# A diffusion trunk on one core: convolution and output product in one block, squares a stage ahead, norms inside the next product stage

## The chip, the core and the metric

The kernel runs on one core of a Trainium2 chip. The metric is the device time of one execution in microseconds (us); several executions are timed and the median is given. TensorE (PE) multiplies matrices, VectorE (DVE) and ScalarE (ACT) do elementwise work, GpSimd (POOL) does a little of it and issues gathers, SyncE (SP) issues transfers. The engines run their own instruction streams and meet at semaphores.

## The reference, cut to what matters

The input is 512 latent tokens and 256 context tokens of 1024 channels, in float32. There are two layers. Each layer is a token mixer followed by a retrieval of experts, and around each stands the same frame:

```python
def rms_norm(x, g):
    xf = x.astype(jnp.float32)
    y = xf * lax.rsqrt(jnp.mean(xf * xf, axis=-1, keepdims=True) + RMS_EPS)
    return (y * g.astype(jnp.float32)).astype(x.dtype)

def modulate(h, shift, scale):
    return h * (1 + scale) + shift
...
def short_conv_mixer(h, w_in, k, w_out, rows):
    gate_b, gate_c, v = jnp.split(h @ w_in, 3, axis=-1)
    z = gate_c * v
    ...
    return (gate_b * zc) @ w_out
...
        hx = modulate(rms_norm(x, norm1_g[i]), mx[0], mx[1])
        ...
        x = x + mx[2] * yx
        x = x + mx[5] * peer_ffn(modulate(rms_norm(x, norm2_g[i]), mx[3], mx[4]),
                                 peer_w_q[i], peer_keys[i], peer_u[i], peer_v[i])
```

The mixer of layer 0 is the short convolution above, that of layer 1 a gated linear recurrence (HGRN2) with eight heads. The experts are found by ranking scores of queries against 128 keys per list, 16 lists a token; the shifts, scales and gates (`mx`, `mc`) come from a product of a condition vector with `ada_w`, 6144 values for each layer and each of the two kinds of token. The output is the final RMS norm of the latent tokens.

## The kernel before, in words

The residual stream `xT` stays in SBUF, channels on the 128 partitions, as 8 slices (k) of 768 tokens (512 in the second half of layer 1). Every big product is taken from weights in tiles of 128 output channels. A tile's weights are loaded to one of four slots (`t.load`, line 129), copied to a rounded high part by ScalarE (`t.hi`, line 133), and the rest is subtracted into a low part by GpSimd or VectorE (`t.lo`, line 144). `t.product` (line 159) then multiplies high by high, high by low and low by high for each k and each bank of up to 512 tokens: 48 matmuls for a tile of 768 tokens. Two accumulators in PSUM alternate; a product waits for `acc_free`, which whoever reads the accumulator out raises. Two sets of split weights alternate too.

The kernel is a sequence of stages. Each stage is a block, and no engine starts the next before all have ended this one:

- `stage_front` (line 199): constants, the modulation of layer 0, the first norm.
- `stage_conv` (line 513): 24 tiles (n), three for each of eight channel slices c, in the order gate c, v, gate b. A loop of two turns has twelve tiles written out in each. ScalarE copies the first accumulator (line 578), VectorE multiplies the second onto it (z, line 616), applies three taps (lines 623 and 632), multiplies the third (y, line 638) and subtracts the part that ScalarE rounded (y_hi, line 583) to get y_lo (line 643). Between these steps VectorE also takes the modulation of layer 1: 48 rows, six for each c, three after z and three after y_lo. A row is 1024 weights on each partition; two dot products (line 608) reduce it against the two condition vectors, with a transfer of 512 KB into one of six slots ahead of it. `acc_free` of the third accumulator is raised at line 641.
- `stage_mix_out` (line 660): eight tiles of the output product. ScalarE copies each accumulator (line 696) and VectorE adds it, scaled, to `xT` (line 717). In layer 1 it first splits the heads' output, and the first product follows this slice by slice.
- `stage_norm` (line 414): squares of the eight slices by ScalarE (line 441) and VectorE (line 468) in turn, sums over partitions by a product of each with a matrix of ones (line 458), root (line 443), reciprocal (line 470). Then VectorE scales each slice (line 484), ScalarE adds the shift and rounds it to `h_hi` (line 450), and VectorE subtracts to get `h_lo` (line 494). It stands three times between other stages (before the first ranking, the recurrence and the second ranking), and a form of it ends the kernel, with the scaled output stored (lines 474 and 504).
- `stage_rank` (line 725): loads the keys (line 751), waits for them (line 763), takes the first query product, then turns the summed h of the sparse tokens (`turn_h`, line 765; ScalarE's copy is line 820) and goes through 16 lists: product, scores, ranks by VectorE.
- `stage_gates` (line 874): dense products against all experts and the gates' matrices. It is not touched.
- `stage_experts` (line 1265): 128 tiles accumulated in all eight PSUM banks, while VectorE adds gathered rows for the sparse tokens. At its end VectorE adds the eight accumulators to `xT` (line 1442), TensorE turns the row sums (line 1364) and VectorE adds these (line 1449).
- `retire` (line 106), after layer 0: GpSimd clears the semaphores used so far.
- `stage_hgrn` (line 1457): the recurrence, 40 tiles, five for each head. Its first five products stand before the loop over heads.

The order around the change is written out by hand, in each engine's stream. Waits are counted in turns; nothing is planned by a program.

Of the kernel before, what the change touches and what calls it, by code (L numbers as in the profile page):

```python
# [23 lines left out]
P = 128  # L24
D = 1024
# [388 lines left out]
def stage_norm(t, layer, n, tokens):  # L414

    nc = t.nc
    final = n == 2
    tag = f"n{layer}{n}"
    hv = banks(tokens)
    segs = [(0, SEQ, 0)] + ([(SEQ, CTX, 1)] if tokens == TOK else [])  # L420
    with ExitStack() as ctx:
        sb = lambda nm, s, d=F32: ctx.enter_context(nc.sbuf_tensor(nm + tag, s, d))
        sq = sb("sq", [P, 2, tokens])
        rs = sb("rs", [P, tokens])
        rstd = sb("rstd", [P, tokens])
        xn = sb("xn", [P, 3, tokens])
        out = sb("out", [P, KC, tokens]) if final else None
        sq_done = [t.sem(f"sq{s}{tag}") for s in ("_act", "_dve")]
        sum_part, root, rstd_done = (t.sem(s + tag) for s in ("sums", "root", "rstd"))
        xn_done, hi_done, lo_done = (t.sem(s + tag) for s in ("xn_", "hi_", "lo_"))  # L430
        stored = t.sem("stored" + tag) if final else None
        h_hi, h_lo = (t.h_hi, t.hc_hi), (t.h_lo, t.hc_lo)
        shift = lambda k, c: t.mod[:, layer, c, 24 * n + k:24 * n + k + 1]
        with nc.Block() as block:  # L434

            @block.scalar
            def _(act):
                for k in range(0, KC, 2):
                    if k >= 2:
                        act.wait_ge(sum_part, k - 1)  # L440
                    act.activation(sq[:, 0], t.xT[:, k, 0:tokens], ACT.Square).then_inc(sq_done[0], 1)  # L441
                act.wait_ge(sum_part, KC)
                act.activation(rs[:], t.acc(0, tokens), ACT.Sqrt, bias=t.eps[:],  # L443
                               scale=1.0 / D).then_inc(root, 1)
                if final:
                    return
                for k in range(KC):
                    act.wait_ge(xn_done, len(segs) * (k + 1))
                    for t0, w, c in segs:
                        act.activation(h_hi[c][:, k], xn[:, k % 3, t0:t0 + w], ACT.Identity,  # L450
                                       bias=shift(k, c)).then_inc(hi_done, 1)

            @block.tensor
            def _(pe):
                for k in range(KC):
                    pe.wait_ge(sq_done[k % 2], k // 2 + 1)
                    for i, (t0, w) in enumerate(hv):
                        last = pe.matmul(t.psum[:, i, 0:w], t.ones[:], sq[:, k % 2, t0:t0 + w],  # L458
                                         start=(k == 0), stop=(k == KC - 1))
                    last.then_inc(sum_part, 1)  # L460

            @block.vector
            def _(dve):
                for k in range(1, KC, 2):
                    if k >= 2:
                        dve.wait_ge(sum_part, k - 1)
                    x = t.xT[:, k, 0:tokens]
                    dve.tensor_tensor(sq[:, 1], x, x, ALU.mult).then_inc(sq_done[1], 1)
# [3 lines left out]
                if final:  # L472
                    for k in range(KC):
                        dve.scalar_tensor_tensor(out=out[:, k], in0=t.xT[:, k, 0:tokens],  # L474
                                                 scalar=t.gains[:, 4, k:k + 1], in1=rstd[:], op0=ALU.mult,
                                                 op1=ALU.mult).then_inc(xn_done, 1)
                    return
# [1463 lines left out]
```

## Time and profile before

| | us |
|---|---|
| median of three executions | 4391.62 |
| lowest, highest | 4388.56, 4394.60 |
| the profiled execution's own time | 4389.09 |
| its span in the profile | 4387.4 |
| mean granted TensorE clock | 0.956 of full |

One execution was recorded. Its span runs from the first to the last instruction; the time has some 2 us around it. Times in rows of a timeline are us from the start of the span: first the start, then the duration (of several instructions of one kind in a row, from the first start to the last end), then engine and line of the kernel, the operation, what it writes and reads, and in brackets how long the engine had been idle and what released it. A name such as DVEq or PEq as the releaser is that engine's sequencer, so a wait for a semaphore or a barrier.

### The profile page before, as it was taken

What the parts mean: (1) busy time and instruction counts of PE and PEld (TensorE: products, weight loads), DVE (VectorE), ACT (ScalarE), POOL (GpSimd) and SP (SyncE); (2) the same over time, 40 slices, a digit from 0 to 9 for tenths busy, and PEclk for the clock granted to TensorE, in tenths of its full rate; (3) what the DMA queues carried; (4) which work ended last, traced back from release to release, by engine and by line L of the source; (5) the groups of instructions that cost most, each with busy time, mean ns of one, the idle gap of its engine ahead of it and who ended that gap; (6) DMA issues with size and microseconds to landing.
All of it is one profiled execution on the core that took longest, in us unless ns stands there. A gap on an engine that the chain in (4) does not pass through costs nothing. (4 is left out here: it accounts for less than half of the span.)

```text
span 4387.4 us, 62475 instructions
## 1 busy us (share of the span) xinstructions
PE 4032.8 (92%) x20380; PEld 3434.4 (78%) x20380; DVE 3231.5 (74%) x5929; ACT 1947.7 (44%) x3694; POOL 1163.9 (27%) x906
## 2 busy tenths in 40 slices
PE   8997788999999989999987999888799999899998
PEld 2776577788888868888866877656789999899997
DVE  2694588999897778888875455546887877577777
ACT  2111224777777722222224434323367778533332
POOL 0232121343343244444422111112122222122221
PEclk9998899999999999999998999889899999999999
DMA  7441115899999899999951111012378888899996
GB/s 278 169 168 58 44 43 183 284 326 335 318 344 332 316 386 375 373 374 376 376 196 49 38 38 39 29 48 77 123 270 285 285 281 300 293 333 333 331 336 213
DMA packets 411888, 1026.08 MB, mean 234 GB/s; under 512 B 33968, under 2 KB 182448, under 8 KB 405680
## 3 DMA queue, kind: packets, MB, share of 16 engines
q1 hardware_dynamic: 297648, 608.42, 39.0%
q0 software_dynamic: 110592, 402.70, 25.7%
q10 hardware_dynamic: 3456, 12.58, 0.9%
q8 instruction: 98, 1.61, 0.1%
q14 instruction: 94, 0.77, 0.1%
HBM read 904.03 MB, written 119.54 MB: 233 GB/s over the span
## 5 line engine op out<-in xcount | busy, mean ns | idle before, releaser
L136 ACT ACTIVATE w_hi<-w_raw 128x1024 fp32r<-128x1024 f32 x536 | 568.1, 1060 | 1197.9 <-PE psum L1354 879.8
L168 PE MATMUL psum<-h_hi,w_hi 128*128 128x512 f32 (+1 forms) x2208 | 876.4, 397 | 140.3 <-DMA keysr<-in_peer_keys 50.0
L169 PE MATMUL psum<-h_lo,w_hi 128*128 128x512 f32 (+1 forms) x2208 | 840.4, 381 | 0.0
L170 PE MATMUL psum<-h_hi,w_lo 128*128 128x512 f32 (+1 forms) x2208 | 839.7, 380 | 0.0
L147 DVE TENSOR_TENSOR w_lo<-w_raw,w_hi 128x1024 fp32r<-128x1024 f32 x424 | 519.5, 1225 | 413.3 <-ACT w_hi L136 392.2
L1352 PE MATMUL psum<-a_hie,w_hi 128*128 128x512 f32 (+1 forms) x2048 | 764.4, 373 | 30.7 <-DVE a_loe L1407 30.7
L1354 PE MATMUL psum<-a_hie,w_lo 128*128 128x512 f32 (+1 forms) x2048 | 751.6, 367 | 0.0
L1353 PE MATMUL psum<-a_loe,w_hi 128*128 128x512 f32 (+1 forms) x2048 | 750.0, 366 | 0.0
L1228 POOL DMA_INDIRECT u_rowsg<-in_peer_u_rows,expert_idx x384 | 443.4, 1155 | 1099.9 <-DVE u_rowsg L985 974.2
L1333 POOL DMA_INDIRECT v_rowse<-in_peer_v,expert_idx x384 | 421.4, 1097 | 828.2 <-DVE row_sume L1416 815.0
L1160 ACT ACTIVATE ojg<-eq_jg,gate_Tg 128x128 fp32r<-128x128 bf16 x1792 | 546.9, 388 | 167.5 <-DVE eq_jg L1008 166.6
L147 POOL TENSOR_TENSOR w_lo<-w_raw,w_hi 128x1024 fp32r<-128x1024 f32 x116 | 289.4, 2495 | 1145.2 <-ACT w_hi L136 1145.2
L168 PEld LDWEIGHTS psum<-h_hi,w_hi 128*128 128x128 f32 x2208 | 425.9, 193 | 195.5 <-issue 84.4
L1416 DVE SCALAR_TENSOR_TENSOR row_sume<-v_rowse,expert_weight,row_sume 128x1024 f32<-128x1024 f32 x384 | 491.4, 1280 | 0.1
L170 PEld LDWEIGHTS psum<-h_hi,w_lo 128*128 128x128 f32 x2208 | 424.3, 192 | 64.8
L985 DVE SCALAR_TENSOR_TENSOR u_rowsg<-u_rowsg,psum 128x1024 f32<-128x1024 f32 x384 | 463.1, 1216 | 9.5 <-DMA u_rowsg<-in_peer_u_rows,expert_idx 6.4
L169 PEld LDWEIGHTS psum<-h_lo,w_hi 128*128 128x128 f32 x2208 | 425.8, 193 | 49.0 <-issue 12.9
L1352 PEld LDWEIGHTS psum<-a_hie,w_hi 128*128 128x128 f32 x2048 | 385.7, 188 | 93.6 <-DVE a_loe L1407 31.8
L1354 PEld LDWEIGHTS psum<-a_hie,w_lo 128*128 128x128 f32 x2048 | 385.7, 188 | 50.4
L1353 PEld LDWEIGHTS psum<-a_loe,w_hi 128*128 128x128 f32 x2048 | 386.1, 189 | 45.9
L1124 PEld LDWEIGHTS psum<-ojg,eq_ig 128*128 128x128 f32 x1792 | 230.9, 192 | 78.8 <-ACT ojg L1160 70.1
L1124 PE MATMUL psum<-ojg,eq_ig 128*128 128x128 f32 x1792 | 232.6, 273 | 50.1 <-ACT ojg L1160 49.9
(228 smaller groups left out, 5740.2 us busy)
## 6 DMA issues: line engine op xcount, KB each, us to landing
w_raw<-in_peer_u SPq DMA_DIRECT2D x256, 512.0 KB, 5.9
w_raw<-in_peer_v SPq DMA_DIRECT2D x256, 512.0 KB, 5.5
gates<-stageg SPq DMA_DIRECT2D x28, 2048.0 KB, 15.7
acts<-act_gg SPq DMA_DIRECT2D x128, 256.0 KB, 5.0
gte<-gates SPq DMA_DIRECT2D x32, 1024.0 KB, 8.3
act_fe<-acts SPq DMA_DIRECT2D x128, 256.0 KB, 6.3
ada_w<-in_ada_w SPq DMA_DIRECT2D x12, 2048.0 KB, 8.2
ada_rows<-in_ada_w SPq DMA_DIRECT2D x48, 512.0 KB, 3.4
```

Source lines behind the costliest of these rows:

```text
L136: act.activation(self.weights(s)[0], self.raw[:, slot, :], ACT.Copy).then_inc(self.hi_done, 1)
L147: pool.tensor_tensor(lo, self.raw[:, slot, :], hi.bitcast(F32), ALU.subtract).then_inc(self.lo_done, 1)
L168: pe.matmul(out, wh, hi[:, k], start=(k == 0), stop=False)
L169: pe.matmul(out, wh, lo[:, k], start=False, stop=False)
L170: last = pe.matmul(out, wl, hi[:, k], start=False, stop=(k == KC - 1))
L985: dve.scalar_tensor_tensor(out=row, in0=row, scalar=1.0, in1=h_row, op0=ALU.mult, op1=ALU.mult, accum_out=pre_act[:, s, r:r + 1]).then_inc ...
L1124: last = pe.matmul(t.psum[:, 4 + g % 2, j * P:(j + 1) * P], eq_i[:, g % EQ, j], oj[:, g % OJ, x, j], start=(x == 0), stop=(x == 1))
L1160: last = act.activation(oj[:, g % OJ, x, j], eq_j[:, g % EQ, j], ACT.Copy, scale=gate_T[:, b % 2, x, r + j:r + j + 1])
L1352: pe.matmul(out, vh, a_hi[:, s], start=(begin and i == 0), stop=False)
L1353: pe.matmul(out, vh, a_lo[:, s], start=False, stop=False)
L1354: last = pe.matmul(out, vl, a_hi[:, s], start=False, stop=(end and i == QUAD - 1))
L1416: dve.scalar_tensor_tensor(out=acc[:, s], in0=vbuf[:, slot], scalar=weight[:, s, bass.ds(c, 1)], in1=acc[:, s], op0=ALU.mult, op1=ALU.add) ...
```

## The change

It has five parts.

1. **Convolution and output product in one block.** `stage_conv` takes N = 32 tiles: 24 as before, then the eight of the output product, the first of them slice by slice behind y_lo. The loops are written out. `stage_mix_out` is no longer called in layer 0.
2. **Modulation rows spread over both.** Four rows for each channel slice (two for the last, and two behind it), then 3, 3, 3, 3, 2, 2, 0, 0 rows in the eight output tiles: 48 as before. One bias addition and the two scale computations stand behind the last row.
3. **Squares taken a stage ahead.** A new class `Squares` lets ScalarE square each slice of `xT` once it has been added to, and VectorE add the squares up; a single product with ones gives the totals. `stage_experts` squares too, but sums with a product for each slice.
4. **Norms applied in the next product stage.** A new class `Normed` holds root, reciprocal, scaling and rounding. `stage_rank` and `stage_hgrn` call it at their start, and their first product waits for each slice.
5. **The turning of h** in `stage_rank` moves from behind the first product into the last four lists. The wait for the keys moves behind the first product.

The core of the diff:

```diff
+class Normed:
+    def scalar(self, act):
+
+        act.activation(self.rs, self.sums, ACT.Sqrt, bias=self.t.eps[:], scale=1.0 / D).then_inc(self.root, 1)
+        for k in range(KC):
+            act.wait_ge(self.xn_done, len(self.segs) * (k + 1))
+            for t0, w, c in self.segs:
+                act.activation(self.h_hi[c][:, k], self.xn[k % 3][:, t0:t0 + w], ACT.Identity,
+                               bias=self.shift(k, c)).then_inc(self.hi_done, 1)
...
+    def ready(self, pe, k):
+        pe.wait_ge(self.lo_done, len(self.segs) * (k + 1))
+
+class Squares:
+    def square(self, act, added, m, count):
+
+        act.wait_ge(added, count)
+        if m >= 3:
+            act.wait_ge(self.ss_done, m - 2)
+        act.activation(self.sq[m % 2] if m else self.ss[:], self.t.xT[:, m, 0:self.tokens],
+                       ACT.Square).then_inc(self.sq_done, 1)
+
+    def add(self, dve, m):
+
+        dve.wait_ge(self.sq_done, m + 1)
+        if m > 1:
+            dve.wait_ge(self.ss_done, m - 1)
+        dve.tensor_tensor(self.ss[:], self.ss[:], self.sq[m % 2], ALU.add).then_inc(self.ss_done, 1)
+
+    def total(self, pe):
+
+        pe.wait_ge(self.ss_done, KC - 1)
+        for b, (t0, w) in enumerate(banks(self.tokens)):
+            pe.matmul(self.t.psum[:, 6 + b, 0:w], self.t.ones[:], self.ss[:, t0:t0 + w], start=True, stop=True)
...
@@ stage_conv
+    ROWS_C = 4
+    ROWS_M = (3, 3, 3, 3, 2, 2, 0, 0)
...
+                for i in range(n):
+                    t.product(pe, i, i % SPLIT, t.moving(T))
+                for k in range(KC):
+                    pe.wait_ge(ylo_done, k + 2)
+                    t.product(pe, n, n % SPLIT, y_moving, [k])
+                for i in range(n + 1, N):
+                    t.product(pe, i, i % SPLIT, y_moving)
+                squares.total(pe)
...
+                def mixed(m):
+                    t.wait_product(act, n + m)
+                    if m >= 2:
+                        act.wait_ge(added, 2 * (m - 1))
+                    act.activation(tmp[m % 2], t.acc((n + m) % SPLIT, T), ACT.Copy).then_inc(copied, 1)
+                    act.wait_ge(copied, m + 1)
+                    act.sem_inc(t.acc_free[(n + m) % SPLIT], 1)
+                    if m:
+                        squares.square(act, added, m - 1, 2 * m)
...
+                    ada(ROWS_C // 2)
+                ada(ROWS_C // 2)
+                for m in range(KC):
+                    dve.wait_ge(copied, m + 1)
+                    for t0, w, c in segs:
+                        dve.scalar_tensor_tensor(out=t.xT[:, m, t0:t0 + w], in0=tmp[m % 2][:, t0:t0 + w],
+                                                 scalar=t.mod[:, 0, c, 16 + m:17 + m], in1=t.xT[:, m, t0:t0 + w],
+                                                 op0=ALU.mult, op1=ALU.add).then_inc(added, 1)
+                    if m >= 2:
+                        squares.add(dve, m - 1)
+                    if ROWS_M[m]:
+                        ada(ROWS_M[m])
...
@@ stage_rank, TensorE
-                pe.wait_ge(k_in, 16)
...
-                t.product(pe, 0, 0, t.moving(tokens))
-                turn_h(pe)
+                for k in range(KC):
+                    norm.ready(pe, k)
+                    t.product(pe, 0, 0, t.moving(tokens), [k])
+                pe.wait_ge(k_in, 16)
...
                 for i in range(n - BODY, n):
+                    if i - (n - BODY) < S:
+                        turn_h(i - (n - BODY))
                     if i + 1 < n:
                         t.product(pe, i + 1, (i + 1) % SPLIT, t.moving(tokens))
...
@@ stage_experts, TensorE
+                for d in range(KC):
+                    if d == 3:
+                        for s in range(S):
+                            turn(s)
+                    total(d, sq[:, d % 2], sums[:, 0:Td])
+                for d in range(KC):
+                    total(KC + d, sq_rows[:, d % 2].rearrange("p s x -> p (s x)"), sums[:, Td:tokens])
...
@@ stage_hgrn, TensorE
-                for i in range(PER):
+                for k in range(KC):
+                    norm.ready(pe, k)
+                    tile(0, 0, 0, [k])
+                for i in range(1, PER):
                     tile(0, 0, i)
```

`Normed.vector` is the part of `stage_norm` from line 469 to line 496, unchanged. In the recurrence its five buffers are buffers that the first head does not need yet.

## Rows read from the trace of the kernel before

**Rows 1.** The page: busy time of each engine.

```profile
PE 4032.8 (92%) x20380; PEld 3434.4 (78%) x20380; DVE 3231.5 (74%) x5929; ACT 1947.7 (44%) x3694; POOL 1163.9 (27%) x906
```

**Rows 2.** Timeline of TensorE: start us, us, engine line op, [idle before].

```profile
117.95 0.79 PE L168 MATMUL psum<-h_hi,w_hi 128*128 128x512 f32 x1 [4.26 <-PEq L238]
...
364.34 0.76 PE L168 MATMUL psum<-y_hi,w_hi 128*128 128x512 f32 x1 [22.51 <-PEq L542]
...
482.93 0.79 PE L168 MATMUL psum<-h_hi,w_hi 128*128 128x512 f32 x1 [29.32 <-DMA keysr<-in_peer_keys]
...
492.88 1.04 PE L771 MATMUL psum<-ident,h_sumr 128*128 128x128 f32 x8
...
495.94 0.48 PE L168 MATMUL psum<-h_hi,w_hi 128*128 128x512 f32 x1
...
2991.67 0.48 PE L168 MATMUL psum<-h_hi,w_hi 128*128 128x512 f32 x1
```

**Rows 3.** Waits of TensorE, 118 to 364 us: us, times, longest.

```profile
PE psum L168 <- DVEq L641: 13.5, 7, 3.4
```

**Rows 4.** Groups of VectorE, 118 to 364 us: the dot products of the modulation.

```profile
L608 DVE CUSTOM_DVE_ANT_0 ada_rows<-ada_rows,cond_rows 128x1024 f32<-128x1024 f32 x48 | 97.9, 2040 | 0.0
...
L608 DVE CUSTOM_DVE_ANT_0 ada_product<-ada_rows,cond_rows 128x1024 f32<-128x1024 f32 x48 | 63.9, 1331 | 9.7 <-DVE ada_dots L608 6.0 <-DVE z L616 3.8
```

**Rows 5.** Timeline of VectorE, and one row of GpSimd, convolution and output product.

```profile
136.94 0.96 DVE L616 TENSOR_TENSOR z<-gate_c,psum 128x768 f32<-128x768 f32 x1 [22.00 <-PE psum L170]
...
142.44 1.23 DVE L608 CUSTOM_DVE_ANT_0 ada_product<-ada_rows,cond_rows 128x1024 f32<-128x1024 f32 x1 [0.19 <-DVE ada_dots L608]
...
145.01 1.23 DVE L608 CUSTOM_DVE_ANT_0 ada_product<-ada_rows,cond_rows 128x1024 f32<-128x1024 f32 x1 [0.19 <-DVE ada_dots L608]
...
349.28 0.62 DVE L623 TENSOR_SCALAR zc<-z,kern 128x768 f32<-128x768 f32 x1
...
354.49 0.96 DVE L643 TENSOR_TENSOR y_lo<-y,y_hi 128x768 f32 x1 [1.03 <-ACT y_hi L583]
...
385.95 2.69 DVE L717 SCALAR_TENSOR_TENSOR xT<-mix,mod,xT 128x512 f32<-128x512 f32 x2 [5.79 <-ACT mix L696]
...
385.30 2.39 POOL L147 TENSOR_TENSOR w_lo<-w_raw,w_hi 128x1024 fp32r<-128x1024 f32 x1 [6.09 <-ACT w_hi L136]
```

**Rows 6.** Windows: us, busy of five engines, PEclk, DMA, at the output product's start.

```profile
364.00:368.00 4.00, 3.66 (x11) 3.11 (x12) 0.00 (x0) 0.00 (x0) 0.00 (x0) 0.50 0.71 247
...
370.00:372.00 2.00, 2.00 (x13) 1.73 (x12) 0.00 (x0) 0.00 (x0) 0.00 (x0) 1.00 0.00 0
```

**Rows 7.** Timelines of ScalarE and VectorE around the first norm.

```profile
450.58 1.28 ACT L443 ACT_TABLE_LOAD   x1
...
454.58 4.95 DVE L470 RECIPROCAL rstdn<-rsn 128x768 f32<-128x768 f32 x1 [2.58 <-ACT rsn L443]
...
476.74 0.48 DVE L494 SCALAR_TENSOR_TENSOR hc_lop<-xnn,mod,hc_hip 128x256 fp32r<-128x256 f32 x1
```

**Rows 8.** The same around the norm ahead of the recurrence.

```profile
2268.99 5.36 DVE L1442 SCALAR_TENSOR_TENSOR xT<-psum,mod,xT 128x512 f32<-128x512 f32 x8 [3.44 <-PE psum L1354]
...
2285.46 0.96 DVE L468 TENSOR_TENSOR sqn<-xT 128x768 f32<-128x768 f32 x1 [6.98 <-PEq L108]
...
2300.61 4.95 DVE L470 RECIPROCAL rstdn<-rsn 128x768 f32<-128x768 f32 x1 [2.58 <-ACT rsn L443]
...
2335.36 0.81 ACT L1679 ACTIVATE f<-psum 128x768 f32<-128x768 f32 x1 [10.34 <-PE psum L170]
```

**Rows 9.** VectorE around the norm ahead of the second ranking.

```profile
2948.67 2.45 DVE L717 SCALAR_TENSOR_TENSOR xT<-mix,mod,xT 128x512 f32<-128x512 f32 x1 [2.92 <-ACT mix L696]
...
2963.03 3.35 DVE L470 RECIPROCAL rstdn<-rsn 128x512 f32<-128x512 f32 x1 [1.94 <-ACT rsn L443]
...
2975.66 2.07 DVE L494 SCALAR_TENSOR_TENSOR h_lo<-xnn,mod,h_hi 128x512 fp32r<-128x512 f32 x3
```

**Rows 10.** TensorE ahead of the last norm's root.

```profile
4365.05 10.16 PE L458 MATMUL psum<-sqn,ones 128*128 128x512 f32 x16 [5.20 <-ACT sqn L441]
```

More of the change, by code:

```diff
@@ L416, in stage_norm, with stage_final @@
+def stage_final(t, sums):
     nc = t.nc
[L417 to L420, printed above, removed]
     with ExitStack() as ctx:
[L422 to L433, printed above, removed]
+        sb = lambda nm, s: ctx.enter_context(nc.sbuf_tensor(nm, s, F32))
+        rs, rstd, out = sb("rs_end", [P, SEQ]), sb("rstd_end", [P, SEQ]), sb("out_end", [P, KC, SEQ])
+        root, rstd_done, out_done, stored = (t.sem(x + "_end") for x in ("root", "rstd", "out", "stored"))
@@ L437, in _ @@
             def _(act):
[L438 to L460, printed above, removed]
+                act.activation(rs[:], sums, ACT.Sqrt, bias=t.eps[:], scale=1.0 / D).then_inc(root, 1)
             @block.vector
             def _(dve):
[L464 to L468, printed above, removed]
                 dve.wait_ge(root, 1)
@@ L586, in _ @@
                 act.activation(cond[:], cond[:], ACT.Silu).then_inc(cond_done, 1)
-                for i in range(n):
+                for i in range(N):
                     t.hi(act, i + SPLIT, (i + SPLIT) % RAW, i % SPLIT, (i + SPLIT) // RAW)
-                    if i + RAW + 1 < n + RAW:
+                    if i + RAW + 1 < N + RAW:
                         load(i + RAW + 1)
-                    evac(i)
+                    if i < n:
+                        evac(i)
+                    else:
+                        mixed(i - n)
+                squares.square(act, added, KC - 1, 2 * KC)
             @block.vector
@@ L660, in stage_mix_out @@
+                squares.add(dve, KC - 1)
+                assert done[0] == 48
+        t.end_stage(N, RAW)
+        return squares.sums
 def stage_mix_out(t, layer, w_name, tokens, moving, nxt, ready=RAW, y=None):
@@ L699, in evac @@
                     act.sem_inc(t.acc_free[i % SPLIT], 1)
+                    if i:
+                        squares.square(act, added, i - 1, len(segs) * i)
                 if y is not None:
@@ L705, in _ @@
                     evac(i)
+                squares.square(act, added, KC - 1, len(segs) * KC)
             @block.vector
@@ L795, in _ @@
             def _(act):
+                norm.scalar(act)
                 act.sem_inc(s_done, 1)
@@ L1502, in stage_hgrn @@
         S = {x: t.sem("h_" + x) for x in names}
+        norm = Normed(t, ctx, LAYER, 0, TOK, sums, [x[:] for x in (e[0], e[1], b[0], b[1], kk[0])])
         def turns(eng, turn):
```

296 lines of the change are left out of this document (162 added, 134 removed).

## The prediction

> **What bounds the kernel now.** I read the busy shares first [rows 1]: TensorE is busy for 92% of the span, so little can be won inside the long product stages, and the question is where its missing 8% (some 350 us) lies. Then the timeline of TensorE at the seams between blocks [rows 2]. It shows a gap of 22.5 us between the convolution's last product and the output product, and 29.3 us between the first norm's sums and the ranking's first product, the sums themselves lying between them and the output product. The same norm returns before the recurrence and before the second ranking, and a shorter one ends the kernel. Last, the waits of TensorE inside the convolution [rows 3]: seven waits, 13.5 us, for the accumulator that VectorE frees at line 641. So in the convolution VectorE is the bound, at the seams it is whatever the barrier waits for, and everywhere else the change touches nothing.
>
> **VectorE in the convolution.** A modulation row is two dot products of 1.23 us, started 2.57 us apart from row to row [rows 5]. Their means of 2.04 and 1.33 us [rows 4] are longer: 161.8 us in all against 96 x 1.23 = 118.1. The surplus, 43.7 us over the 24 weight subtractions that GpSimd does there, is 1.8 us for each; one lasts 2.39 us, and the additions of the output product that meet one take 2.69 us [rows 5]. I charge VectorE 2.0 us for each GpSimd subtraction; the bounds are 1.8 and 2.4. A channel then costs z and its hop 1.5, six rows 15.4, taps, y and y_lo 6.2 (349.28 to 355.45) [rows 5], three subtractions 6.0: 29.1 us. TensorE needs three products of 2.69 + 5.79 = 8.48, the period of the output product's additions [rows 5]: 25.4 us. With four rows VectorE needs 24.0, and TensorE becomes the bound with 1.4 us in hand. Two products are done when the first z starts, at 136.94; 22 more of 8.48 end at 323.3, where before they ended at 341.83 (the start at 364.34 less its wait [rows 2]).
>
> **The joined block.** The output product's first tile now follows at once, since its last slice needs y_lo some 3 us after 323.3 and reaches it 7.4 us after. TensorE could be done 67.8 us later, but VectorE cannot. From 323.3 on it has: y and y_lo 3.1; 4 rows left in the convolution and 16 in the output product, 20 x 2.57 = 51.4; eight pairs of additions, 1.24 a pair when nothing blocks them (8 x 1.24 = 9.9); seven additions of squares, priced as the 0.96 of the same shape [rows 5] with a hop, 7.4; modulation, scales and hops 2.5; nine GpSimd subtractions, 18; the last square on ScalarE 1.0. Sum 93.3. This is the one place where the change moves the bound: TensorE will wait for accumulators (ScalarE's copy waits for the addition two tiles back, and its square for the one before) in the last two or three tiles. One total of 768 columns follows. The last norm's sums took 10.16 us for 8 x 512 columns [rows 10], 1.9 us for 768, and part of that stretch was at the full clock; behind a wait I take 2.6. Then barrier 0.5, table load 1.28 [rows 7], root 0.9, hops 0.2: the reciprocal starts at 422.1 instead of 454.58 [rows 7], **32.5 us earlier**.
>
> From the reciprocal to the last h_lo took 22.6 us (454.58 to 477.22 [rows 7]) and takes as long, since VectorE sets it. But the first ranking product now runs beside it, slice by slice, and only its last slice (1.06 us, or 2.1 at half clock; I take 1.6) is left: the second product starts at 446.3 where it started at 495.94 [rows 2]. In the 49.6 us lie also the wait for the keys, asked for at the old block's start and now needed a product later, and the two turnings of h for h_tok, 3.1 us before (492.88 to 495.94) [rows 2]. The turnings come back in the last ranking turns as 2 x 1.04, hidden by nothing on TensorE: 2.1. Their copies on ScalarE (about 1 us each) stand ahead of the query copy, which has a whole product's time.
>
> **Clock.** After each seam TensorE runs at 0.50 of full speed, the level of 1.2 GHz, and rises to 2.4 GHz some 5 us into dense work [rows 6]. A product in slices paced by VectorE at 2.24 us (22.6 less reciprocal and start, over eight) is idle for half its time if fast and for a tenth if slow, so I leave 1 us of cold work in the following product; bounds 0 and one whole product at half clock, 8.5 us. First seam: 49.6 - 2.1 - 1.0 = **46.5 us**.
>
> **Ahead of the recurrence.** Before: additions from 2268.99, all done 6.98 us before 2285.46, so at 2278.5 [rows 8]; those 6.98 are the semaphore clearing of line 108, and stay. After: squares and totals start with the first addition. They are the same columns that the norm summed, 8 x 768, plus the two turnings; TensorE needs some 15 us from 2270 at the mixed clock of the old sums, or 11 if it stays fast. I take 2285 for the end (2281 to 2287). Clearing, table load, root: the reciprocal at 2294.4 for 2300.61 [rows 8]. Then 22.6 + 1.6 + 0.3, and the first gate is read at 2319.0 where it was at 2335.36 [rows 8]: 16.4, less 1 for the clock, **15.5 us**. GpSimd's fills now run beside the reciprocal; at most 3 us if they block VectorE.
>
> **Ahead of the second ranking.** The last addition ends at 2951.1 [rows 9]. Square 0.6, addition 0.7, hops 0.3, one total 1.5, barrier 0.5, root 0.8: the reciprocal starts at 2955.6 for 2963.03. The last h_lo came 14.7 us behind it (2975.66 + 2.07 = 2977.73) [rows 9]: 2970.3, and the second product starts at 2971.3 for 2991.67 [rows 2]. 20.4, less 1.4 for clock and turning, **19 us**. In the output product before it the added square (0.6) and addition (0.7) per tile cost nothing: a tile there lasts 2.45 + 2.92 us, with VectorE idle for the 2.92 [rows 9], and ScalarE, with a weight copy and a copy out, is idle for more than half of it.
>
> **The end.** The old sums took 10.16 us behind the last addition [rows 10]. The same columns now overlap 6 us of additions; the table load, once hidden in the wait, shows: **4 us**, bounds 2 and 7.
>
> **Sum.** 46.5 + 15.5 + 19 + 4 = 85. The profiled execution took 4389.1 us (span 4387.4), 2.5 below the median of 4391.6. 4391.6 - 85 = **4306.5**.
>
> The table load lasts 1.28 us in this trace [rows 7]. The Trainium skill (ScalarE: Activation LUTs, What ACT_TABLE_LOAD costs) adds a drain of about 1.38 us to every switch. Three switches come onto the path here, so by the page the result would be 4 us higher; the rows show no such pause, since the engine was waiting anyway.
>
> **The rivals.** (a) *More*: the GpSimd subtractions fall into VectorE's waits, or VectorE holds them off instead, and the totals stay fast: 9 x 1.8 = 16 less, and up to 7 less, so 4290 likely. For it: GpSimd waits for VectorE too where it comes second. Against it: VectorE has no waits of its own in that stretch for a subtraction to fall into. 0.12.
> (b) *The clock*: products in slices never raise it, and each following product runs at half clock: 8.5 + 8.5 + 5.4 less the 2.7 charged, 4326. For it: the level of 0.50 after any gap [rows 6]. 0.12.
> (c) *Absorbed*: the stages behind the later two seams are held by something that does not start earlier (weights loaded, keys), so 34.5 us are not won: 4341. Against it: each gap ends with a block's own start. 0.06.
> (d) *Slower*: the joined block is written out instead of looped, 32 x 48 products on TensorE alone, and the code comes too slowly. It decides from 85 us over 1536 products, 55 ns each; at 100 ns, 154 us are lost and the time is 4461. Against it: the old output product is written out too and keeps 8.48 [rows 5]. 0.04.
> The Trainium skill (SBUF — State Buffer, SBUF: two separate sides) has the port pair of VectorE and GpSimd as an exclusive lock for a whole instruction, so a subtraction would cost up to its 2.39 us, not 2.0: 9 x 0.4 makes 3.5 us more.
>
> **How the numbers follow.** The forecast has 0.66: 4306.5, 4297 to 4316 by its own bounds. The range is 4288 to 4328; it holds it, most of (a) and (b). A measurement can tell 0.2%, some 9 us. Faster: 0.66 + 0.12 + 0.12 + 0.06 less 0.01 = 0.95; same 0.01; slower 0.04.
>
> **What would show it.** Right: no wait at the accumulator inside the convolution, the last convolution product near 323; the first reciprocal near 422, the second near 2248 (46.5 + 6.2 ahead of 2300.6), the third near 2894 (62 + 7.4 ahead of 2963.0); VectorE busy above 95% through the output product. Wrong: TensorE waiting between slices for longer than 2.3 us, half clock for whole products after a seam, dot products whose mean stays over 1.8 us, or a first z later than 137 us.

## The result, and the profile after

| | before | after |
|---|---|---|
| median | 4393.11 (4388.56 to 4396.47, 4 runs) | 4282.85 (4279.37 to 4288.58, 4 runs) |
| ratio | | 0.9758, 95% interval 0.9745 to 0.9772 |
| profiled execution, span | 4389.09, 4387.4 | 4288.58, 4286.9 |
| granted clock | 0.956 | 0.963 |

Faster by 110 us, where 85 were forecast: the median lies 5 us below the low end of the range. Later measurements of the same two kernels gave 4284.07 beside 4390.93 and 4285.52 beside 4386.82, so 101 to 107 us less; over all executions the means are 4388.6 (35 of them) and 4284.2 (13), 104 us apart. Two more profiles were taken of each kernel. The table has the mean of three each, in the order of the program. Its marks are the first z, the first copy of scores in layer 0, the first gelu, the start of the expert additions of layer 0, the first gate f, and so on.

| stretch | before | after | gain | forecast |
|---|---|---|---|---|
| start to first z | 136.4 | 135.2 | 1.2 | 0 |
| first z to first scores | 369.1 | 310.9 | 58.2 | } 46.5 |
| scores to gelu, layer 0 | 163.9 | 165.7 | -1.8 | } |
| gelu to expert additions | 1600.7 | 1597.9 | 2.8 | 0 |
| expert additions to first f | 66.5 | 48.7 | 17.8 | 15.5 |
| first f to last output addition | 613.3 | 608.5 | 4.8 | 0 |
| last output addition to first scores | 49.7 | 29.1 | 20.6 | 19 |
| scores to gelu, layer 1 | 117.2 | 116.0 | 1.2 | 0 |
| gelu to expert additions | 1241.3 | 1247.3 | -6.0 | 0 |
| expert additions to the end | 29.2 | 25.4 | 3.8 | 4 |

The gains add to 102.6, as the spans do (4387.2 less 4284.5), near the 104 of all executions: the 110 of the four-execution medians is some 6 us of spread too high. Against the 85 of the forecast, the profiles have 9.9 us more at the first seam, 2.3 and 1.6 more at the next two, 0.2 less at the end, and 4.0 in stretches that it put at nothing.

The page of the changed kernel, the row that answers to [rows 1]:

```profile
PE 4009.6 (94%) x20354; PEld 3426.2 (80%) x20354; DVE 3233.5 (75%) x5926; ACT 1963.4 (46%) x3726; POOL 1163.7 (27%) x906
```

TensorE's busy time fell by 23 us; at two norms the sums of eight slices became one, and the mean granted clock rose from 0.956 to 0.963. The rest of the gain is idle time taken out.

The waits of TensorE from 110 to 470 us (us, times, longest), for [rows 3]:

```profile
PE psum L499 <- DVE ss_m L493: 18.2, 1, 18.2
PE psum L168 <- DVE hc_lop L462: 14.2, 4, 11.9
```

The wait for the accumulator inside the convolution and the wait at the block's end are gone. What stands there is one wait of 18.2 us for VectorE's sum of squares: VectorE's list is the new bound, as the prediction had it. The waits for accumulators that it expected of TensorE in the last two or three tiles are not there. VectorE's timeline through the joined block, for [rows 5] and [rows 7]:

```profile
134.69 0.95 DVE L663 TENSOR_TENSOR z<-gate_c,psum 128x768 f32<-128x768 f32 x1 [21.32 <-PE psum L170]
...
160.01 0.95 DVE L663 TENSOR_TENSOR z<-gate_c,psum 128x768 f32<-128x768 f32 x1 [2.35 <-PE psum L170]
...
320.37 0.95 DVE L683 TENSOR_TENSOR y<-zc,psum 128x768 f32<-128x768 f32 x1 [2.35 <-PE psum L170]
322.26 2.52 DVE L687 TENSOR_TENSOR y_lo<-y,y_hi 128x768 fp32r<-128x768 f32 x1 [0.93 <-ACT y_hi L615]
324.70 1.22 DVE L656 CUSTOM_DVE_ANT_0 ada_product<-ada_rows,cond_rows 128x1024 f32<-128x1024 f32 x1
...
330.95 3.42 DVE L656 CUSTOM_DVE_ANT_0 ada_rows<-ada_rows,cond_rows 128x1024 f32<-128x1024 f32 x1
...
336.85 1.15 DVE L693 SCALAR_TENSOR_TENSOR xT<-z,mod,xT 128x512 f32<-128x512 f32 x2
337.91 1.22 DVE L656 CUSTOM_DVE_ANT_0 ada_product<-ada_rows,cond_rows 128x1024 f32<-128x1024 f32 x1
...
361.10 0.95 DVE L493 TENSOR_TENSOR ss_m<-ss_m,y 128x768 f32<-128x768 f32 x1
361.97 1.22 DVE L656 CUSTOM_DVE_ANT_0 ada_product<-ada_rows,cond_rows 128x1024 f32<-128x1024 f32 x1
...
402.75 0.25 DVE L702 TENSOR_TENSOR mod<-ada_dots,ada_bias 128x96 f32<-128x96 f32 x1
403.04 0.26 DVE L194 SCALAR_TENSOR_TENSOR gs<-mod,gains 128x16 f32<-128x16 f32 x2
403.21 1.14 DVE L693 SCALAR_TENSOR_TENSOR xT<-zc,mod,xT 128x512 f32<-128x512 f32 x2
...
405.33 0.96 DVE L493 TENSOR_TENSOR ss_m<-ss_m,y 128x768 f32<-128x768 f32 x1
411.76 4.95 DVE L453 RECIPROCAL own1n<-own0n 128x768 f32<-128x768 f32 x1 [5.47 <-ACT own0n L434]
```

Read the starts, not the durations. A pair of additions is shown with 1.15 us, but the next instruction starts 1.06 behind its start (336.85, 337.91); an addition of squares is shown with 0.95 and takes 0.87 (361.10, 361.97). Before every z but the first, VectorE now waits 2.35 us for TensorE, and 21.3 us before the first.

GpSimd's subtractions in the same stretch:

```profile
321.57 2.40 POOL L147 TENSOR_TENSOR w_lo<-w_raw,w_hi 128x1024 fp32r<-128x1024 f32 x1 [5.66 <-ACT w_hi L136]
330.05 3.23 POOL L147 TENSOR_TENSOR w_lo<-w_raw,w_hi 128x1024 fp32r<-128x1024 f32 x1 [6.08 <-ACT w_hi L136]
```

The second is 0.83 longer than the first, and the dot product that starts at 330.95 takes 3.42 instead of 1.22: GpSimd first waits for the dot product under way, then VectorE waits for GpSimd. Nine such losses lie between 320 and 406 us, 1.56 to 2.24 us each, 18.6 in all: the first is y_lo, 2.52 instead of 0.96, the other eight lie in the output product.

ScalarE and TensorE at the seam, ScalarE's last square of `xT` first:

```profile
404.39 0.84 ACT L485 ACTIVATE y<-xT 128x768 f32<-128x768 f32 x1 [1.55 <-DVE xT L693]
...
409.53 1.28 ACT L434 ACT_TABLE_LOAD   x1 [4.29 <-PEq L572]
410.82 0.90 ACT L434 ACTIVATE own0n<-psum,eps 128x768 f32<-128x768 f32 x1
```

```profile
387.89 0.28 PE L170 MATMUL psum<-y_hi,w_lo 128*128 128x256 f32 x1
406.34 2.93 PE L499 MATMUL psum<-ss_m,ones 128*128 128x512 f32 x4 [18.18 <-DVE ss_m L493]
421.12 0.79 PE L168 MATMUL psum<-h_hi,w_hi 128*128 128x512 f32 x1 [11.85 <-DVE hc_lop L462]
```

And the clock (PEclk is the eighth value, behind the five engines' busy time) while the first ranking product follows the norm:

```profile
421.00:423.00 2.00, 1.88 (x6) 1.59 (x6) 1.96 (x5) 0.88 (x3) 0.00 (x0) 0.50 0.00 0
...
425.00:427.00 2.00, 2.00 (x9) 1.57 (x8) 1.97 (x5) 0.88 (x3) 0.00 (x0) 0.64 0.00 0
427.00:430.00 3.00, 1.63 (x9) 1.08 (x7) 2.96 (x6) 1.88 (x4) 0.00 (x0) 1.00 0.00 0
430.00:436.00 6.00, 4.98 (x26) 4.22 (x27) 5.93 (x11) 1.36 (x4) 0.00 (x0) 1.00 0.01 3
```

At 0.50, the level of 1.2 GHz, a slice fills the time that VectorE needs for the next. From 427 on the clock is 1.00, 2.4 GHz, and the second product starts at that.

### The profile page after: what moved, and what is told of

Read it like the earlier page. It is cut to its first block and busy times, and to the rows that moved or that the text cites. A ratio compares the mean times of both kernels' runs of the same rounds, so it can differ in the third digit from the quotient of the medians.

```text
span 4286.9 us, 62093 instructions
## 1 busy us (share of the span) xinstructions
PE 4009.6 (94%) x20354; PEld 3426.2 (80%) x20354; DVE 3233.5 (75%) x5926; ACT 1963.4 (46%) x3726; POOL 1163.7 (27%) x906
```

## The experiments

In all of them the numbers are medians in us with their range, ratios are to the kernel before, measured beside each. "z to reciprocal" is the stretch from the first z to the start of the reciprocal of the first norm: 317 before (317.6, 316.3 and 317.8 in three profiles), 277.1 in the changed kernel.

**One block and spread rows alone** (parts 1 and 2; squares and norms as before, in blocks of their own):

```diff
-                squares.total(pe)
-        return squares.sums
+  (stage_norm, stage_rank, stage_experts, stage_hgrn of before)
```

> Edit: the kernel before with parts 1 and 2 of the change alone (convolution and output product in one block, rows spread, loops written out); squares, sums and norms stay in blocks of their own. Theory A (the gain is the sum of what happens at the seams): without the seven additions of squares VectorE ends its additions some 79 us behind the last convolution product, so near 399 us where they ended at 439.5; everything behind it keeps its old length. 38 to 40 us faster than before, first reciprocal near 414. Rival B (what the forecast missed is run to run spread, and the parts are worth what it said, 32.5 us for the block): 31 to 33 us faster.

4349.32 (4344.72 to 4353.82), ratio 0.9902 (0.9884 to 0.9920). z to reciprocal 281.4, and behind it nothing but what was there before: reciprocal to first scores 51.6 (before 51.4). So these two parts bring some 36 us at the first seam, 42 by the medians. VectorE's list ends there too: its last additions to `xT` start at 400.29, and end 2.4 us behind the 399 of theory A; the reciprocal starts at 417.4, not near 414. The 42 us are somewhat more than theory A's 38 to 40, and rival B's 31 to 33 are out.

**Squares ahead, but norms in blocks of their own** (part 4 undone, 1, 2, 3 and 5 kept):

```diff
+        with nc.Block() as block:
+            @block.scalar
+            def _(act):
+                norm.scalar(act)
+            @block.vector
+            def _(dve):
+                norm.vector(dve)
+                dve.wait_ge(norm.lo_done, len(norm.segs) * KC)
         with nc.Block() as block:
...
-                norm.scalar(act)
...
-                norm.vector(dve)
```

> Edit: the changed kernel with part 4 undone: root, scaling and rounding stand in blocks of their own again ahead of both rankings and the recurrence; squares are still taken a stage ahead. Theory A: 57 to 62 us faster than before, so slower than the changed kernel by 40 to 50 (two reciprocals stay where the changed kernel has them, and each following product starts a whole product and the block's start later: 14.5, 15.5 and 13 us). Rival B: slower than the changed kernel by 14.9 + 9.2 + 11.5 = 36 us or less, as the forecast had it.

4311.89 (4310.40 to 4312.62), ratio 0.9819 (0.9803 to 0.9836). Against the kernel above, 37 us less: z to reciprocal 4.4 less, the keys and the turning 7.1 (reciprocal to scores 44.5), 5.6 ahead of the second reciprocal, 7.2 ahead of the third, 5.2 behind it, 4 at the end: 33.5. Against the changed kernel, 28 us more: reciprocal to scores 10.7, reciprocal to f 11.0, reciprocal to scores of layer 1 8.0, 29.7 in all. So the overlap of norm and product (part 4) is worth 28 us, less than either of the others (42 for parts 1 and 2, 37 for 3 and 5). Theory A, 40 to 50 us, was too much; the bound of rival B, 36 or less, holds.

**The two kernels again.**

> The changed kernel once more, unchanged, for a second recorded execution. Its first one has 8 us more in the second dense product stage than the kernel before has. Theory A: that is spread of one execution: here the stage is as long as before within 2 us, and the time is near 4283, 108 to 112 us below before. Rival C (the change itself lengthens that stage, by another placement of buffers or phase of transfers): 8 us again.

> The kernel before once more, for a second recorded execution. Theory A: the start of the first product, the recurrence's heads and the dense stages move by up to 3 us each against the first recording; the seams do not move by 0.3 us. Rival C: the stages repeat to 0.5 us, and what differs between the two kernels outside the seams is the change's doing.

4284.07 (4281.58 to 4286.29), ratio 0.9758 (0.9741 to 0.9774), and 4395.33. z to reciprocal again 277.1, expert additions to f again 48.7. The long dense stages are what differs between two executions: gelu to expert additions in layer 0 was 1598.9 and 1607.4 in two profiles of the same kernel before. In layer 1 the stretch was 1246.5 in this execution of the changed kernel, 4.5 us above the first profile of the kernel before: neither the 2 of theory A nor the 8 of rival C. The seams repeat less well than theory A had it (0.3 us): z to reciprocal moved by 1.3 us in the kernel before.

**All rows in the convolution.** Six for each channel, none in the output product:

```diff
-    ROWS_C = 4
-    ROWS_M = (3, 3, 3, 3, 2, 2, 0, 0)
+    ROWS_C = 6
+    ROWS_M = (0, 0, 0, 0, 0, 0, 0, 0)
```

> Edit: the changed kernel with all 48 modulation rows in the convolution again, six a channel slice. Theory A: VectorE bounds the convolution again, its last product ends 204.9 us behind the first z as before (now 185.5), but the output product then runs at TensorE's pace of 8.48 us a tile: the last addition of squares ends near 277 us behind the first z for 271.6 now. 5 to 6 us slower than the changed kernel, so the spread itself is worth little. Rival E (the spread is what makes the joined block pay): 15 us slower or more.

4295.22 (4293.79 to 4297.07), ratio 0.9787 (0.9764 to 0.9810): 11 us more than the changed kernel, where 5 to 6 were expected, 7.3 of them from z to reciprocal (284.4). TensorE's old wait is back inside the convolution, and the new one ahead of the totals falls from 18.2 to 6.5:

```profile
PE psum L168 <- DVEq L685: 12.8, 7, 3.0
PE psum L499 <- DVE ss_m L493: 6.5, 1, 6.5
```

So joining the blocks is worth most of the seam, and the spreading of the rows 7 us there; the other 4 lie outside it, where the dense stages differ from one execution to the next.

**No rows in the output product, and none instead**: sixteen modulation rows are left out, so their time is missing too.

```diff
-    ROWS_M = (3, 3, 3, 3, 2, 2, 0, 0)
+    ROWS_M = (0, 0, 0, 0, 0, 0, 0, 0)
...
-                assert done[0] == 48
+                assert done[0] == 32
```

> Edit: the changed kernel without the 16 modulation rows of the output product (the last 16 of the 48 rows of layer 1's modulation are left out and set to zero). It measures what VectorE's lag behind TensorE costs in the joined block. Theory A: the block ends with TensorE: 185.5 + 67.8 + 4.5 = 258 us behind the first z for 271.6, 13 to 14 us faster. Rival F (the block is held by TensorE's or ScalarE's own chain, squares included): 0 to 4 us faster.

4274.17 (4269.82 to 4276.49), ratio 0.9735 (0.9712 to 0.9758). z to reciprocal 265.4, 11.7 less where 13 to 14 were expected, although 16 x 2.46 = 39 us of VectorE's work are gone. The rest TensorE decides. Its wait ahead of the totals is 6.5 us here too: copy, addition, square and addition of the last tile. That is the floor of this seam, and 11.7 us is all that a lighter list can win.

**The weight subtractions of the output product on VectorE**, not GpSimd:

```diff
-                for i in range(SPLIT, N + SPLIT):
+                for i in range(SPLIT, n + SPLIT):
                     t.lo(pool, i, i % RAW, i % SPLIT)
...
                     dve.wait_ge(copied, m + 1)
+                    t.lo(dve, n + m + SPLIT, (n + m + SPLIT) % RAW, (n + m) % SPLIT)
```

> Edit: the changed kernel with the eight weight subtractions of the output product on VectorE instead of GpSimd (line 147, behind the wait for the copied accumulator). Theory A (each GpSimd subtraction costs VectorE about 2.06 us by blocking it): VectorE then pays 1.14 us each instead, no dot product of the output part is longer than 1.25 us, and the block ends 4 to 7 us earlier. Rival G (the long dot products come from something else, the rows' transfers): dot products of 3.4 us stay, and the block ends 9 us later.

4277.35 (4275.34 to 4282.15), ratio 0.9748 (0.9724 to 0.9771); z to reciprocal 270.2, 6.9 less. VectorE does eight more subtractions and is sooner done. The groups of VectorE from 323 to 406 us, first the changed kernel, then this one:

```profile
L656 DVE CUSTOM_DVE_ANT_0 ada_rows<-ada_rows,cond_rows 128x1024 f32<-128x1024 f32 x20 | 35.4, 1772 | 0.0
L656 DVE CUSTOM_DVE_ANT_0 ada_product<-ada_rows,cond_rows 128x1024 f32<-128x1024 f32 x20 | 28.3, 1417 | 2.3 <-issue 2.3
```

```profile
L656 DVE CUSTOM_DVE_ANT_0 ada_product<-ada_rows,cond_rows 128x1024 f32<-128x1024 f32 x20 | 24.5, 1223 | 2.3 <-issue 2.3
L656 DVE CUSTOM_DVE_ANT_0 ada_rows<-ada_rows,cond_rows 128x1024 f32<-128x1024 f32 x20 | 24.4, 1220 | 0.0
L147 DVE TENSOR_TENSOR w_lo<-w_raw,w_hi 128x1024 fp32r<-128x1024 f32 x8 | 9.8, 1221 | 1.0 <-ACT zc L621 1.0
```

A subtraction costs VectorE 1.14 us from start to start if it does it itself, and 2.14 on average (the eight losses in the output product) if GpSimd does it beside it: 8 x (2.14 - 1.14) = 8.0, less 1.0 of new waiting, is 7.0, beside the 6.9 measured. Rival (a) of the prediction is out by this: the subtractions do not fall into waits, they cost what was charged. TensorE in its turn now waits for the subtracted weights, which is most of what is left above the 265.4 of the kernel without the rows:

```profile
PE psum L499 <- DVE ss_m L493: 6.2, 1, 6.2
PE psum L168 <- DVE w_lo L147: 4.3, 3, 1.7
```

**The turning first**, where it was (part 5's move undone, the later wait for the keys kept):

```diff
+                for s in range(S):
+                    turn_h(s)
                 pe.wait_ge(k_in, 16)
...
-                    if i - (n - BODY) < S:
-                        turn_h(i - (n - BODY))
```

> Edit: the changed kernel with the turning of h and its copies behind the first ranking product again. Theory A: the first score comes 3 us later in the first ranking and 1.5 in the second, and the last lists give back 2.4 us in the first: 2 us slower in all, at the edge of what can be told. Rival: the keys or the sum of h make TensorE wait longer there, 5 us or more.

4288.22 (4286.84 to 4293.57), ratio 0.9774 (0.9750 to 0.9798). Reciprocal to first scores 37.1 instead of 33.8, and in layer 1 1.3 later. From the first scores to the first gelu it is 163.5 instead of 165.5 to 166.2, so the move wins 3.3 us and gives 2.0 to 2.7 back (the prediction charged 2.1), which leaves about 1 us at layer 0 and 1.3 at layer 1. The rival's wait of 5 us or more is not there. The medians lie some 4 us apart, at the edge of what can be told.

**Early rows.** VectorE is idle for 21 us before the first z. Five rows ahead of it, eleven instead of sixteen in the output product:

```diff
+    LEAD_ROWS = 5
+    ROWS_C = ((1, 3), (2, 2), (2, 2), (2, 2), (2, 2), (2, 2), (2, 2), (0, 4))
+    ROWS_M = (2, 2, 2, 2, 2, 1, 0, 0)
...
+                dve.sem_inc(ada_done, 2 * ADA_SLOTS + 1)
                 dve.wait_ge(k_in, 32)
                 dve.wait_ge(cond_done, 1)
-                dve.sem_inc(ada_done, 2 * ADA_SLOTS + 1)
...
+                ada(LEAD_ROWS)
```

> Five modulation rows are taken by VectorE ahead of the first z, in the 21 us in which it has nothing to do there, and eleven stay in the output part instead of sixteen (the other 32 still lie in the convolution). Theory (the first seam of the changed kernel is set by VectorE's list in the joined block): five rows by about 2.5 us leave the part behind the last z, so the reciprocal behind the squares comes 10 to 12.5 us sooner (z to reciprocal from 277 to about 266), and the kernel takes about 4272 us. Rival 1 (TensorE's own end of the output product and not VectorE's list is nearly as late: the kernel without the sixteen rows won 10 to 12 us): the gain stops at that floor, about 4273. Rival 2 (the early rows' transfers and the wait for them hold up the first z, since the weights' transfers run at the same time): the first z comes 2 to 10 us later, and the kernel takes 4275 to 4283 us.

4271.77 (4268.13 to 4276.94), ratio 0.9743 (0.9729 to 0.9756). The reciprocal starts at 401.0 (413.1 and 411.8 in the changed kernel), and the wait of TensorE ahead of the totals is the floor's:

```profile
124.57 1.23 DVE L657 CUSTOM_DVE_ANT_0 ada_product<-ada_rows,cond_rows 128x1024 f32<-128x1024 f32 x1 [11.21 <-ACT cond_rows L629]
...
141.22 0.94 DVE L665 TENSOR_TENSOR z<-gate_c,psum 128x768 f32<-128x768 f32 x1
```

```profile
395.59 2.93 PE L499 MATMUL psum<-ss_m,ones 128*128 128x512 f32 x4 [6.50 <-DVE ss_m L493]
```

The first z is 6 us later, as rival 2 had it (2 to 10 us), though not for want of transfers but because the fifth row ends only at 141.2: the condition vector that a row needs is ready at 124.6, so that only some 12 of the 21 us are open, and two GpSimd subtractions fall among the rows. It costs nothing, since the last z is at 312.9, as in the changed kernel (311.9 to 313.2): the 2.35 us of idle time in each channel make it up.

**Six early rows**, 35 in the convolution, 7 in the output product, and the same with the subtractions on VectorE:

```diff
+    LEAD_ROWS = 6
+    ROWS_C = ((0, 4), (2, 2), (2, 3), (2, 2), (2, 3), (2, 2), (2, 3), (0, 4))
+    ROWS_M = (2, 1, 1, 1, 1, 1, 0, 0)
```

> Six modulation rows ahead of the first z, 35 in the convolution (three channels carry one more) and seven in the output part. Theory: nine rows fewer behind the last z would be 22 us, but the kernel without rows there shows that the seam has a floor at about 265 us from the first z to the reciprocal, which TensorE sets; so z to reciprocal about 266, as with five, and three channels of the convolution that become up to 2.5 us longer where VectorE had 2.35 us idle: about 0 to 2 us given back; about 4272 to 4275 us. If VectorE's list were all that counts, it would be 4262 us.

> The rows as in the kernel with six ahead, and the eight weight subtractions of the output part on VectorE instead of GpSimd. If the floor of the seam is TensorE's, moving the subtractions brings nothing more (265 us from z to reciprocal, about 4272 us), or costs up to 3 us, since the rounded weights now wait for VectorE's turn. If GpSimd's hold on VectorE is still in the way, another 3 to 7 us go, and it takes about 4266 us.

4277.30 (4274.59 to 4280.47), ratio 0.9752 (0.9738 to 0.9766), and 4277.53 (4272.52 to 4281.52), ratio 0.9754 (0.9740 to 0.9767). The reciprocal starts at 402.3 and 402.4, with TensorE's wait ahead of the totals 6.5 and 6.2: the floor holds, and moving the subtractions adds nothing to it. Both medians are 5 us above the kernel with five rows and above the 4272 to 4275 that were expected. Only 1.3 us of this come from this seam; the rest lies in the dense stages.

**The changed kernel, the five early rows and the kernel before once more**, beside each other.

> The changed kernel once more, on the same chip and in the same rounds as the kernel with five early rows. If the first seam is worth what the other profiles show, the stretch from the first z to the first score product of layer 0 is again 311 us (before 369), and the dense layers between are again anywhere within their spread: gates of layer 0 at 857 to 862 us, gates of layer 1 at 677 to 680. If the change lengthened layer 1's gates for good, it is again 677 or more, where the kernel before shows 672; if not, they overlap.

> Five early rows, beside the changed kernel. Theory: 10 to 12 us less than the changed kernel of the same rounds, with the first score product about 9 us sooner. Rival: the lower time of the first measurement was half a faster chip (the kernel before also took 4386 us there, where it took 4390 to 4393 elsewhere), and the gain is 5 to 7 us, or within 0.2%.

> The kernel before once more, for its profile alone: whether its gates of layer 1 stay at 672 us (then the 677 to 680 of the changed kernel is the change's doing) or spread as far, and whether its last recurrence takes 96.5 us from the last f to the last o again (92 to 93 in most profiles with the change's parts).

After: 4285.52 (4279.45 to 4289.74), ratio 0.9764 (0.9751 to 0.9778). Five rows: 4275.46 (4269.39 to 4279.94), ratio 0.9747 (0.9734 to 0.9761). Before, one execution: 4382.45. The means of these five executions each lie 9.6 us apart; in all, 13 executions of the changed kernel have a mean of 4284.2 and ten of the one with five rows 4273.7, 10.5 us less with a 95% interval of 3 us either way. The first scores come at 434.1 instead of 445.7. So the kernel with five early rows is the fastest of this study, about 2.6% below the kernel before.

Layer 1's gates (first to last gelu) took 675.4 us in the changed kernel and 672.1 in the kernel before: less than the 677 that would have shown a lasting loss, and yet no overlap. The last f to the last o took 94.9 in the kernel before, and not again 96.5.

## Why the prediction was wrong, and where it was right

**Right: what bounds each seam.** The last convolution product ended near 320, VectorE and not TensorE set the end of the joined block, and the gains of parts 3 and 4 came where they were put. The time is nearest to rival (a), but its mechanism is not there: the subtractions cost what was charged (18.6 for 18.0), and the totals ahead of the recurrence won less than 1 us over the forecast (from the first addition to the reciprocal 24.7 us for 25.4), where the rival had up to 7 for all totals. One detail failed that cost nothing in the sum: TensorE never waited for an accumulator in the last tiles. VectorE was busy for 97% of the output product, as forecast (above 95), in the windows of five engines:

```profile
323.00:388.00 65.00, 65.00 (x370) 56.45 (x368) 63.09 (x81) 16.33 (x19) 19.39 (x8) 1.00 0.51 172
388.00:406.00 18.00, 0.17 (x2) 0.00 (x0) 17.50 (x27) 4.17 (x5) 2.65 (x2) 0.62 0.00 0
```

The third value is VectorE's: 63.09 of 65, and 17.50 of 18 while TensorE stands still. The first is TensorE's: 65.00 of 65, so its eight tiles ran without a wait, and all of the waiting came behind them. By its own marks: second reciprocal at 2233.9 (2248 forecast), third at 2872.9 (2894), 14 and 21 us early: mostly what the first seam had gained more, then 2 us of the second seam and what the recurrence gave, below. The seams behind the first were forecast within 3 us: 17.8 for 15.5, 20.6 for 19, 3.8 for 4.

**Wrong: the sum of VectorE's list in the joined block.** This is the step that failed. The prediction had the list end at 323.3 + 93.3 = 416.6; it ended at 406.3. It began at 320.4, 2.9 us earlier (2.25 of them from an earlier first z), and lasted 86.0 us. The step by its terms, in us, measured by the starts in the whole timeline, of which rows are shown above:

| term | forecast | measured |
|---|---|---|
| y and y_lo | 3.1 | 2.8 |
| 20 rows | 51.4 | 49.2 |
| 8 pairs of additions | 9.9 | 8.5 |
| 7 additions of squares | 7.4 | 6.4 |
| modulation, scales, hops | 2.5 | 0.5 |
| nine GpSimd subtractions | 18.0 | 18.6 |
| last square of ScalarE | 1.0 | 0 |
| sum | 93.3 | 86.0 |

All but one err the same way, for three reasons. Additions and squares were priced by their durations, while consecutive instructions of VectorE that wait for nothing overlap by 0.09 us here: 15 x 0.09 = 1.3. Hops and small terms were put on top, 4 us of them, and lay under other work: ScalarE's squares were ready when VectorE came to them, and even the last ended at 405.2, as VectorE's addition before it did. And the row was priced from row to row, 2.57, which holds only between rows; the last of a group takes 2.30, so 2.46 on average: 2.2. The GpSimd charge, with its bounds of 1.8 and 2.4 each, was right to 0.6 us in all.

The rest of the first seam: a tile took 8.44 us and not 8.48, 0.9 us over 22, less 0.2 for a slip of the prediction (136.94 + 22 x 8.48 is 323.5, not 323.3); from reciprocal to second product 23.8 for 24.2; the charge of 1.0 for the clock did not come; the turnings cost 1.8 for 2.1. 7.3 + 0.9 - 0.2 + 0.1 (the reciprocal followed the list's end by 5.4, not 5.5) + 0.4 + 1.0 + 0.3 is 9.8 of the 9.9 by which this seam beat its forecast (58.2 - 1.8 against 46.5).

**Wrong: the charges for the clock**, 1.0, 1.0 and a part of 1.4. The prediction left some cold work for the product behind a sliced one. The windows above show 1.00 from 427 on, before the sliced product is half done: what is slow is hidden by VectorE's pace, and nothing is left for the product behind it. This term had the bounds 0 and 8.5; the value was 0. Rival (b) had put it near the other bound.

**The table load** took 1.28, and the root started 0.01 behind its end, as the sum had it. The Trainium skill (ScalarE: Activation LUTs, What ACT_TABLE_LOAD costs) has a drain of about 1.38 us with every switch; this trace does not show one. The reason that the prediction gave, that the engine was waiting anyway, is not it: at 1011.57, where ScalarE was busy, the load stands 0.02 us behind the instruction before it and 0.01 ahead of the next.

**Not forecast: some 5 us in the recurrence, 6 given back in layer 1's gates.** From the last f to the last o (ScalarE's copy of a head's output, line 1727 of the kernel before) the kernel before took 96.6, 96.4 and 94.9, the changed one 92.3, 93.1 and 92.9. It goes with the clock in the last head's 80 or so small products. The windows of 17 us before the last o, of the kernel before, of the changed one, and of the one with the turning first:

```profile
2873.00:2890.00 17.00, 14.39 (x81) 14.04 (x80) 2.14 (x8) 0.32 (x1) 0.00 (x0) 0.67 0.00 0
```

```profile
2790.00:2807.00 17.00, 14.42 (x86) 12.04 (x86) 5.34 (x20) 0.00 (x0) 0.00 (x0) 0.86 0.01 1
```

```profile
2794.00:2811.00 17.00, 14.80 (x82) 13.91 (x81) 3.01 (x12) 0.00 (x0) 0.00 (x0) 0.69 0.01 1
```

Nothing in these products was touched. The kernel with the turning first has all of the change's other parts and takes 96.6 again, while the one with parts 1 and 2 alone takes 92.1, and every other kernel with parts of the change 92.3 to 93.1. The granted clock goes with it, 0.67 and 0.69 against 0.86; what makes it fall in one kernel and not in another was not tested.

Layer 1, first gelu to the expert additions, took 1240.8 to 1242.0 in three profiles of the kernel before and 1245.2 to 1250.1 in three of the changed one. The five early rows, which have all of the change, take 1243.3 and 1243.9, and no kernel with a part of it is below 1242.9. So every version with a part of the change lost about 1 us at least, though the gates' code was not touched, and the rest varies within 1243 to 1250. What sets it stays open.

**The range.** Its low end, 4288, lies 18.5 us below the forecast. It took in rival (a) at 4290, though that rival with all of its terms comes to 4306.5 - 16 - 7 = 4283.5. The errors did not cancel: the list (7.3), the clock (up to 3.4) and what was not forecast (4.0) all went one way, and the four-execution medians added some 6 us of spread. The mean of all 13 executions, 4284.2, lies below the range as well, by 4 us.

## What to carry to other kernels

Price a list of instructions on one engine from start to start within the trace, taking the stretch of the densest same mix, and add a hop only where the timeline shows a wait for it; durations, hops and a price that held only between rows made the list 8% too long here. When a change moves the bound to another engine, compute the floor that the first engine keeps (here 6.5 us of tail behind the last tile): it says how much a lighter list can still win, and where to stop. And look for the engine's idle time ahead of a bound stretch: five rows before the first z, where VectorE was idle for 21 us, brought 10 us. Whether one more row in each channel of the convolution would have done the same was not run. With six early rows, a channel that carried five rows took 25.5 to 25.7 us against 25.32, so by an estimate from these rows it would cost some 2 us there and take 8 x 2.46 = 20 from the list, more than the floor lets through.

## What was not expected of the hardware

GpSimd's subtraction (2.40 us) costs VectorE 1.6 to 2.2 us each time, and the order in which the two meet decides who waits, 0.83 us of 3.23 on GpSimd's side in the row at 330.05. The Trainium skill (SBUF — State Buffer, SBUF: two separate sides) has the shared port pair as a lock held for the whole instruction. The rows agree: each loss is somewhat under the 2.40, and in the row at 330.05 GpSimd's time grew while a dot product was under way. Where VectorE was the bound, the slower engine's help was a loss, 2.14 us of waiting against 1.14 of its own; with six early rows, where TensorE set the end, moving the subtractions brought nothing.

TensorE's clock rose from 0.50 to 1.00 in the middle of a product paced by VectorE, at 427 where the first slice had started at 421.12. The same stands ahead of the recurrence (first slice at 2243.24, clock 1.00 from 2250 to 2256) and ahead of the second ranking (0.50 from 2879 to 2882, 1.00 from 2886 to 2891).
